# A decoder step on one Trainium2 core: another first norm, two projection units side by side, and five gate units moved to the end of the convolution

## What is computed

```python
def conv_mixer(x, prev, norm_g, w_in, conv_w, conv_b, ln_g, ln_b, w_out):
    h = rms_norm(x, norm_g)
    a, b, z = jnp.split(h @ w_in, 3, axis=-1)
    u = a * jax.nn.sigmoid(b)
    u_ext = jnp.concatenate([prev.astype(u.dtype), u], axis=1)
    c = lax.conv_general_dilated(...) + conv_b          # causal, depthwise, width 31
    c = jax.nn.silu(layer_norm(c, ln_g, ln_b))          # norm over all 2048 channels
    out = (c * jax.nn.silu(z)) @ w_out
    return out, u_ext[:, -(CONV_W - 1):]
```

## Time and profile before

| | us |
|---|---|
| median of three runs | 2424.27 (2417.22 to 2424.91) |
| the profiled execution | 2416.76 |
| its span in the trace | 2414.9 |
| what lies around the span | 1.9 |
| PE busy | 2209.6 (91%) |
| DVE / ACT / POOL busy | 1313.2 (54%) / 940.2 (39%) / 1069.7 (44%) |

### The profile page before, as it was taken

How to read it: one execution, slowest core, us unless ns; L and a number is a source line. 1 busy time by engine, 2 the same in 40 slices (tenths; PEclk the granted TensorE clock), 3 DMA queues, 4 the chain that set the end, 5 groups by cost and what they waited for, 6 DMA issues and landing times.

```text
span 2414.9 us, 46942 instructions
## 1 busy us (share of the span) xinstructions
PE 2209.6 (91%) x16540; PEld 1908.8 (79%) x16540; DVE 1313.2 (54%) x1892; ACT 940.2 (39%) x1617; POOL 1069.7 (44%) x715
## 2 busy tenths in 40 slices
PE   5999999999458997979999999988999998989999
PEld 3999999999347997978999888854555555558998
DVE  4698889889874005574787311113544544545332
ACT  4566566556453003231322112323454444453121
POOL 0688998898766123443333343222222222212130
PEclk7999999999789998989999999988999999999999
DMA  3222222222124112131422579999999999973212
GB/s 114 69 71 76 67 70 76 74 66 76 58 74 163 50 52 87 61 133 66 150 74 89 203 243 335 357 358 397 415 397 397 417 397 397 405 298 113 65 45 84
DMA packets 137489, 430.99 MB, mean 178 GB/s; under 512 B 23889, under 2 KB 40658, under 8 KB 136162
## 3 DMA queue, kind: packets, MB, share of 16 engines
q1 hardware_dynamic: 121554, 375.94, 42.1%
q0 software_dynamic: 13168, 41.58, 4.8%
q10 hardware_dynamic: 2592, 11.14, 1.2%
HBM read 386.81 MB, written 43.87 MB: 178 GB/s over the span
## 4 chain that ended last, share of the span: by engine, by line
PE 53%; POOL 14%; DVE 8%; issue 8%; DMA 6%; ACT 6%; SPq 4%; ACTq 0%; POOLq 0%; DVEq 0%
POOL ACC L1371 7%; PE PS L611 6%; PE PS L613 6%; PE PS L612 6%; PE PS L728 5%; PE PS L730 5%; PE PS L729 5%; PE PS L850 4%; PE PS L794 3%; DMA KV<-cv 3%; POOL WL L1344 2%; PE PS L929 2%; PE PS L619 2%; DMA KV<-ck 2%; SPq L526 2%
## 5 line engine op out<-in xcount | busy, mean ns | idle before, releaser
L1344 POOL TENSOR_TENSOR WL<-RAW,WH 128x1024 fp32r<-128x1024 f32 (+1 forms) x121 | 305.3, 2525 | 575.3 <-ACT WH L979 570.7
L1687 DVE SCALAR_TENSOR_TENSOR PS<-UX,CWT,PS 128x1024 f32<-128x1024 f32 (+1 forms) x672 | 466.3, 782 | 0.0
L644 PE MATMUL PS<-HH,WH 128*128 128x384 f32 (+1 forms) x1152 | 378.5, 329 | 20.7 <-DVE HL L1673 20.7
L646 PE MATMUL PS<-HH,WL 128*128 128x384 f32 (+1 forms) x1152 | 377.4, 328 | 0.0
L645 PE MATMUL PS<-HL,WH 128*128 128x384 f32 (+1 forms) x1152 | 377.2, 327 | 0.0
L1371 POOL TENSOR_TENSOR ACC<-ACC,PROD 128x1088 f32<-128x1088 f32 x112 | 284.7, 2542 | 31.3 <-ACT PROD L1031 25.1
L728 PE MATMUL PS<-GH,WH 128*128 128x384 f32 (+1 forms) x792 | 267.0, 337 | 24.2 <-DVE KC L1812 12.1
L730 PE MATMUL PS<-GH,WL 128*128 128x384 f32 (+1 forms) x792 | 262.5, 331 | 0.0
L729 PE MATMUL PS<-GL,WH 128*128 128x384 f32 (+1 forms) x792 | 261.4, 330 | 0.0
L644 PEld LDWEIGHTS PS<-HH,WH 128*128 128x128 f32 x1152 | 217.3, 189 | 24.7 <-issue 13.7
L979 ACT ACTIVATE WH<-RAW 128x1024 fp32r<-128x1024 f32 (+1 forms) x121 | 131.3, 1086 | 241.8 <-PE PS L613 207.5
(11 more groups left out here) (220 smaller groups left out, 4338.7 us busy)
## 6 DMA issues: line engine op xcount, KB each, us to landing
KV<-ck SPq DMA_DIRECT2D x256, 512.0 KB, 12.2
KV<-cv SPq DMA_DIRECT2D x256, 512.0 KB, 12.6
RAW<-wA SPq DMA_DIRECT2D x48, 512.0 KB, 3.4
RAW<-wP SPq DMA_DIRECT2D x16, 640.0 KB, 4.0
zT_scr<-ZS ACTq DMA_DIRECT2D x16, 544.0 KB, 2.7
Z<-zT_scr SPq DMA_DIRECT2D x16, 544.0 KB, 3.7
RAW<-wB SPq DMA_DIRECT2D x17, 512.0 KB, 3.4
RAW<-wO SPq DMA_DIRECT2D x16, 512.0 KB, 3.5
```

The lines of the kernel that those rows point to most:

```text
L644: pe.matmul(out, WH[w][:, kk], HH[:, k, a:b], start=k == 0, stop=False)
L646: mm = pe.matmul(out, WL[w][:, kk], HH[:, k, a:b], start=False, stop=k == KD - 1)
L1344: pool.tensor_tensor(WL[s][:, 0:n], RAW[s][:, 0:n], WH[s][:, 0:n].bitcast(F32), ALU.subtract).then_inc(s_lo, 1)
L1687: i = dve.scalar_tensor_tensor(out=o, in0=x, scalar=w[:, j:j + 1], in1=o, op0=ALU.mult, op1=ALU.add)
```

## The change

- **First norm.** ACT squares into four buffers `SQ0`; DVE adds the eight squares up in `SS0` (seven additions). PE turns that into nine columns of PSUM (nine matmuls with one column of ones), in which partition p of column c is the sum of row 128c + p. Root and reciprocal work on these nine columns, and `spread` (nine matmuls by the identity) brings the result to all partitions in `CHAIN`, from which DVE multiplies.
- **First two units.** Units 0 and 1 (b and a of chunk 0) run side by side over `PAIR_CH`, k by k, as the low parts arrive.
- **Order of units.** `conv_order` puts no z unit behind the `a` of chunks 0, 4, 8, 12 and 15. The eleven others hold the z units of chunks 0 to 10; those of chunks 11 to 15 stand at the end. So four chunks (0, 4, 8, 12) have two units in them and eleven have three; behind the `a` of chunk 15 run five z units.
- **Rings.** The PSUM slots go round five banks in order.
- **POOL.** `gated(n + 1)` moves ahead of the last addition of chunk n. `CSUM` holds 15 chunks; the last goes into the mean by a second matmul over `CC[:, 15, :]`, in banks 0 to 2 instead of `CHAIN`. Six pair sums are made instead of eight, and the last four tiles of squares go to PE one by one.
- **SP.** The loop is written out. In chunk n stand all weight loads first, and then all twelve pages of `past_logf`.
- **ACT, POOL, PE, SP** have the 16 chunks written out, with no hardware loop; DVE keeps its loop.

```diff
@@ SP
+            for n in range(NCH):
+                s = n % 2
                 sp.wait_ge(s_u, n + 1)
+                sp.dma_start(cpT[n], UX[s][:, USAMP - HIST:USAMP]).then_inc(s_cst, 16)
+                sp.dma_start(csT[n], UX[s][:, USAMP:UEXT]).then_inc(s_cst, 16)
+                if n < NCH - 1:
                     atleast(sp, s_cst, 32 * n)
                     atleast(sp, s_c, n)
+                    sp.dma_start(UX[1 - s][:, USAMP:UEXT], est[n + 1]).then_inc(s_est[1 - s], 16)
+                    sp.dma_start(CWT[1 - s][:], cw[n + 1]).then_inc(s_est[1 - s], 16)
-                for j in (5, 6, 7):
-                    u = 3 * n + j
...
-                    past_logf(i, NPG // 2 * s + 4 * (j - 5), 4)
+                for u in range(a_place[n] + 4, a_place[n + 1] + 4 if n < NCH - 1 else U_OUT + 4):
+                    conv_raw(u)
+                for j in range(3):
+                    past_logf(n // 2, NPG // 2 * s + 4 * j, 4)
@@ order
+        Z_WAITS = (0, 4, 8, 12, 15)
+        conv_order = []
+        for n in range(NCH):
+            conv_order += [(n, 0), (n, 1)]
+            if n not in Z_WAITS:
+                conv_order.append((n - sum(w < n for w in Z_WAITS), 2))
+        conv_order += [(n, 2) for n in range(NCH - len(Z_WAITS), NCH)]
@@ PE
+            pe.wait_ge(s_ss0, KD - 1)
+            for c, n in TOK:
+                mm = pe.matmul(PS[0:n, 0, c:c + 1], SS0[:, P * c:P * c + n], ONES[:, 0:1], start=True, stop=True)
+            mm.then_inc(s_st0, 1)
+            pe.wait_ge(s_inv, 1)
+            spread(SD0).then_inc(s_rs0, 1)
+            pe.wait_ge(s_lo, 2)
             for k in range(KD):
+                pe.wait_ge(s_h, k + 1)
+                for u in range(2):
+                    for r, (a, b) in enumerate(PAIR_CH):
...
+            mean_part(CSUM, True)
             pe.wait_ge(s_c, NCH)
+            mean_part(CC[:, NCH - 1, :], False).then_inc(s_mmu, 1)
@@ ACT
+            for n in range(NCH):
+                s, u = n % 2, a_place[n] + 1
+                three = n == NCH - 1 or a_place[n + 1] == u + 2
+                conv_hi(u + 1)
                 product(n, s, 0)
                 product(n, s, 1)
+                empty(u, 0)
                 product(n, s, 2)
+                empty(u, 1)
                 product(n, s, 3)
+                empty(u, 2)
+                conv_hi(u + 2)
                 product(n, s, 4)
+                if three:
+                    empty(u + 1, 0)
+                    product(n, s, 5)
...
+                else:
+                    product(n, s, 5)
+                    product(n, s, 6)
+                    empty(u + 1, 0)
...
@@ POOL
+            gated(0, 0)
+            for n in range(NCH):
+                s, u = n % 2, a_place[n] + 1
+                lo(u + 1, (u + 1) % 2)
+                if n > 0:
+                    csum(n - 1)
                 adds(n, s, range(1, 3))
+                lo(u + 2, (u + 2) % 2)
                 adds(n, s, range(3, 6))
+                if n == NCH - 1 or a_place[n + 1] == u + 2:
+                    lo(u + 3, (u + 3) % 2)
+                adds(n, s, range(6, NT - 1))
+                if n < NCH - 1:
+                    gated(n + 1, 1 - s)
+                adds(n, s, range(NT - 1, NT))
@@ DVE
+            dve.wait_ge(s_sq0, 2)
+            dve.tensor_tensor(SS0[:], SQ0[0][:], SQ0[1][:], ALU.add).then_inc(s_ss0, 1)
+            for k in range(2, KD):
...
+                dve.tensor_tensor(SS0[:], SS0[:], SQ0[k % 4][:], ALU.add).then_inc(s_ss0, 1)
```

More of the change, by code:

```diff
@@ L141, in build @@
         T0 = [m(f"T0{s}", [P, R]) for s in range(2)]
[L142 removed]
+        SQ0 = [m(f"SQ0{s}", [P, R]) for s in range(4)]
+        SS0 = m("SS0", [P, R])
+        SD0 = m("SD0", [P, NT])
         m = Map(at_x)
@@ L624, in _ @@
             pe.wait_ge(s_con, 32)
-            for k in range(KD):
[L626 to L647, removed]
@@ new lines, in _ @@
+            for u, (n, kind) in enumerate(conv_order):
+                if u < PAIRED:
+                    continue
+                pe.wait_ge(s_lo, u + 1)
+                for r, (a, b) in enumerate(RCH):
+                    g = 3 * u + r
+                    atleast(pe, s_eva, max(g - 4, 6) if u == PAIRED > 0 and r > 0 else g - 4)
+                    out = PS[:, slot_bank(g), 0:b - a]
+                    for k in range(KD):
+                        kk = slice(k * P, (k + 1) * P)
+                        pe.matmul(out, WH[u % 2][:, kk], HH[:, k, a:b], start=k == 0, stop=False)
+                        pe.matmul(out, WH[u % 2][:, kk], HL[:, k, a:b], start=False, stop=False)
+                        mm = pe.matmul(out, WL[u % 2][:, kk], HH[:, k, a:b], start=False, stop=k == KD - 1)
+                    mm.then_inc(s_slot, 1)
@@ L651, in _, with mean_part @@
+            def mean_part(src, first):
+                for a, b in PAIR_CH:
+                    mm = pe.matmul(MEAN[:, a:b], ONES, src[:, a:b], start=first, stop=not first)
+                return mm
+            pe.wait_ge(s_csum, NCH)
             pe.wait_ge(s_eva, 9 * NCH)
+            mean_part(CSUM, True)
             pe.wait_ge(s_c, NCH)
-            for a, b in ((0, 512), (512, 1024), (1024, R)):
-                mm = pe.matmul(CHAIN[:, a:b], ONES, CSUM[:, a:b], start=True, stop=True)
@@ L1056, in chunk @@
                 product(n, s, 4)
[L1057 to L1067, removed]
@@ L1075, in _ @@
+            for u in (U_OUT - 2, U_OUT - 1):
+                conv_hi(u + 1)
+                for r in range(3):
+                    empty(u, r)
+            conv_hi(U_OUT + 1)
             act.wait_ge(s_mmu, 1)
@@ L1378, in csum @@
                 pool.tensor_tensor(CSUM[:], CSUM[:], src, ALU.add).then_inc(s_csum, 1)
[L1380 to L1384, removed]
+            gated(0, 0)
[3 more added lines that the diff above has]
+                if n > 0:
                     csum(n - 1)
                 adds(n, s, range(1, 3))
-                lo(3 * n + 4, (s + 4) % 2)
+                lo(u + 2, (u + 2) % 2)
                 adds(n, s, range(3, 6))
[L1389 to L1395, removed]
+                if n == NCH - 1 or a_place[n + 1] == u + 2:
[4 more added lines that the diff above has]
+                adds(n, s, range(NT - 1, NT))
+            for u in range(U_OUT - 1, U_OUT + 2):
+                lo(u, u % 2)
+            for p in range(6):
                 pool.wait_ge(s_sq1, 2 * p + 2)
```

157 lines of the change are left out of this document (95 added, 62 removed).

## The result

| | before | after |
|---|---|---|
| median of 15 runs each | 2417.75 us (2412.36 to 2424.91) | 2431.76 us (2426.65 to 2435.3) |
| profiled execution's span | 2414.9 us | 2424.8 us |

The ratio after to before is 1.0054, with a 95% interval of 1.0045 to 1.0063: 13 us slower by the ratio, 14.0 by the medians. The forecast was 2440 where the kernel before stood at 2424.27 by three runs, so 1.0065; the range of 2428 to 2454 held the time. Two executions, one of 3854.9 us of the kernel before (beside e9) and one of 5140.2 us of e7, lie far outside all others and are in no ratio.

What follows compares the result with a forecast made beforehand. PE was full in the loop, POOL nearly so. Chunk 1 start 97.7, eleven chunks of 35.3, three of 41.3, 0.5 and an end of 56.0 put the mean at 666.4, +15.5 with squares: 2440 us, range 2428 to 2454.

Steps and rivals of the forecast that it cites:

- Start: First norm and first two units: T0 at 27.5 instead of 33.98, first taps at 67.1 instead of 78.94, 11.8 us earlier.
- the 2.5 us for the low clock: Units 0 and 1 side by side: time added for a block at half speed, range 1.8 to 3.5 us.
- Three-unit chunks: Chunks with a z unit in the loop: POOL sets the pace at 35.3 us each, eleven of them.
- Rival 3: Loop: POOL's own gaps shrink by up to 0.8 us in each of 11 chunks, 2431 us; chance 0.08.
- Two-unit chunks: Chunks 4, 8, 12: late load holds the sigmoid and product 2, POOL 8.9 us late, 41.3 us instead of 32.4.
- the table load of 1.28 us: ACT in two-unit chunks: counted between the load's landing at 14.7 and the sigmoid of 0.4 us.
- O + 5.8: Latest load landing without delay in a two-unit chunk; O is the end of the previous chunk's last addition.
- rival 1: Two-unit chunks: loads come in time, three chunks take 32.4 us, 26.7 us less, 2413 us; chance 0.14.
- Rival 2: Three-unit chunks: the page burst delays them too, 0.7 us in each of seven, 2450 us; chance 0.12.
- The end: Behind the start of chunk 15 (O15): z units end at 51.3, mean at 56.0; squares 0.3 us more.
- The sum: Whole kernel: mean at 666.4 against 651.2, +15.2 us, with the squares +15.5; 2440 us on the median.
- the half microsecond for chunk 0: Chunk 0: 0.5 us added because its `cw` load arrives just in time.

Runs made afterwards that it cites:

- e9: Kernel before with the new first norm alone, units 0 and 1 behind each other as before: 0.9967 of the kernel before.
- e7: e3 with SP's loop of 16 chunks written out: 1.0004 of the kernel before.
- e1: Changed kernel with SP's twelve pages again in fours, each four behind a weight load: 2404.62 us, 0.9949 of the kernel before.
- e3: Kernel before with all three weight loads first, then the twelve pages, in SP's queue: 1.0107 of the kernel before.
- e8: Changed kernel with pages between loads, three z units at the end and eight pair sums instead of six and four single: 0.9901 of the kernel before.
- e6: Kernel before with the changed front alone (new first norm, units 0 and 1 side by side): 0.9945 of the kernel before.

## Why the prediction was right, point by point

- **Start.** `T0` was forecast at 27.5 and came at 27.34; the first matmul at 31.5, came at 31.30; the nine column sums and the spread, 4 and 4.3 us, took 3.85 and 4.40, nearer to the low-clock estimate than to the bound of 2.3 worked out from the transposes. PE started unit 2 at 62.43 where 63.4 follows from the text: the 2.5 us for the low clock were too much. The matmuls ran at half pace (0.43 us from one to the next, later 0.23) only from 31.3 to 34.5, one block's worth, 1.5 us by the forecast's own rows. In e1 they did so until 37.7, and unit 2 began 1.2 us later behind its first matmul. First taps: 67.1 forecast, 65.88 measured.
- **Three-unit chunks.** 35.3 forecast, 35.12 on average (386.4 us over eleven): POOL's own time, and PE no longer seen. This term, elevenfold, was 1.9 us too long. Rival 3, by which POOL's gaps would shrink, did not come: POOL's wait before the second addition is 1.50 us in every three-unit chunk, where it was 1.59.
- **Two-unit chunks.** The mechanism came as told, in the three chunks named, link by link: SP free 11.0 us into the chunk (forecast 11.3), ACT standing, POOL late. Of POOL's 9.30 us of idle time in chunk 4, 1.50 are there in e1 too, so it was 7.8 us late (forecast 8.9). Without the delay 32.4 was forecast, and e1 has 32.28. With it 41.3 was forecast and 39.9, 41.4, 39.9 measured. The step that was mis-sized is the table load of 1.28 us ahead of the sigmoid, which the forecast had put behind the wait. It isn't there: in such a chunk no z unit has changed ACT's table since the last sigmoid. (The forecast's terms also add up to 17.8, not 17.95.) For the same reason the load may come later than the O + 5.8 of rival 1, at some O + 7.1: ACT waits 5.8 us there before the chunk gets longer, as 13.40 us of wait and 7.63 of length show. The middle chunk has a burst of 20.96 us where the others have 19.68, and so a longer time: with it the table load's error is hidden in chunk 8, which is luck.
- **Rival 1** (loads in time) is the kernel e1. It was worked out at 26.7 us under the forecast; e1 is at 0.9949 where the changed kernel is at 1.0054, 25 us. The time that a sequencer takes to initiate a DMA is "usually small relative to the DMA itself" (the Trainium skill, DMA: Bandwidth & Descriptors, Issuing engines are not separate DMA queues); for the pages the trace does not agree: each took 1.64 us of SP's time in a row of twelve, and such a page lands in 2.0 us. That its place would hardly matter was the forecast's conclusion from this; e1 against the changed kernel shows that it was worth 1%.
- **Rival 2** (the burst reaches three-unit chunks) did not come in the changed kernel, but came in e3, where the bursts were 22.3 to 24.16 us. The cover was read too small. The forecast took the 1.93 us of the earlier trace rows, of which a load at 14.7 leaves 1.1; e3 and e7 show 3.2 us. So the changed kernel was safer there than forecast, and the 0.7 us that rival 2 gave each three-unit chunk, for a wait of 2.6 us, wouldn't have come. In the changed kernel ACT's table load also runs ahead of this wait in three-unit chunks, and not behind it as in e3 and e7.
- **The end.** The last spread was forecast 56.0 behind the start of chunk 15 and took 57.35 (604.19 to 661.54). The squares took 2.0 us more than before (36.99 for 34.94) instead of 0.3: the form with four single sums, under a clock of 0.86, as the rows at e8 show.
- **The sum.** Forecast at the mean +15.2, measured +10.3: the start -1.1, the eleven chunks -1.9, the three chunks -2.7, the half microsecond for chunk 0 that wasn't needed -0.5, the end +1.35. With the squares +15.5 was forecast at the reciprocal and +12.3 measured. The span is 9.9 us longer and the median of many runs 14; the runs of one kernel are 9 to 13 us apart, and the profiled one is the fastest of the changed kernel's fifteen. That 15.5 lies so near to 14 is partly luck: by the profile the stages gave less. And the 2440 stood on a median of three runs that lies 6.5 us above that of fifteen.
- **What the forecast did not see** although its rows had it: that the reordering is worth nothing even without the delay. It gave the end 9 us beside the 11.8 of the front, but its own rival 1, with the loads in time, comes to 2413, 11 us under the kernel before, which is the front alone. In e6 the front alone is as fast as e1. The reason stands in the forecast's own numbers: five z units end at O15 + 51 and DVE at O15 + 33, so 18 us of the tail were idle time for everybody but PE. Against the old order (e6) chunk 15 starts 15.9 us sooner after the first taps in e1, and the tail gives 16.6 back.

## What to carry to other kernels

Where an engine's queue only issues transfers, treat each issue as an instruction with a duration, and ask for every load behind a block of them who wants it first: here each chunk's two loads had 20 us of page issues ahead of them, and in three chunks that held up the engine that set the pace. When work is moved to fill a gap at the end of a loop, move as much as fills it and no more; of the counts tried, the best is where both engines end nearly together, which two rows of the timeline give (three units, not five, 0.9895 against 0.9949). And a chunk with one step less needs its loads sooner: here ACT came to the sigmoid 1.3 us into a two-unit chunk and some 14 into a three-unit one.

## What was not expected of the hardware

- Twelve small DMA issues in three short loops took SP 19.7 us (at times up to 21.1) in written-out code and 22.3 to 24.16 us inside an outer hardware loop; four between other issues there took 6.46 us.
- Eighteen passes of fp32 matmuls with a single moving column took 3.85 us, 0.21 each, hardly less than 0.24 for those with 128 columns: at the front of this kernel small matmuls cost by the piece, not by the column.
- At the front PE's matmuls of 512 columns ran at half pace at first, 0.43 us from one to the next, then at 0.23. In the changed kernel that lasted 3.2 us, in e1, which differs only in SP's queue, 6.2. From 28 to 60 us the view shows a granted clock of 1.00 in the one and 0.89 in the other, so the 1.00 doesn't show the short slow piece.
